# Pair scores of eight GLA heads: the levels within 32 tokens as 32x32 blocks in one round

## The chip, the cores and the metric

One core of a Trainium2 chip runs the whole program in one launch. The metric is the device time of one execution in microseconds (us), the median of several runs. TensorE is written PE, VectorE DVE, ScalarE ACT, GpSimd POOL, and SyncE, which issues most DMAs, SP.

## The reference, cut to what matters

The model is a two-layer streaming encoder: 1024 prompt tokens and 8 x 16 sample tokens, width 1024. Layer 0 mixes tokens with two recurrences side by side, a gated DeltaNet and a GLA (gated linear attention) with 8 heads of key width 32 and value width 64. The change concerns the pairwise part of GLA inside one block of tokens:

```python
b = jnp.cumsum(gc, axis=2)
diff = b[:, :, :, None, :] - b[:, :, None, :, :]
decay = jnp.exp(jnp.where(causal[:, :, None], diff, -jnp.inf))
a = jnp.einsum('bhid,bhjd,bhijd->bhij', qc, kc, decay)
o = o_inter + jnp.einsum('bhij,bhje->bhie', a, vc)
```

For each pair of a query i and a key j not after it the score is the sum over 32 channels of q, k and a decay that depends on both and on the channel. `o_inter` is what comes from the carried state. All data are float32.

## The kernel before, in words

The program runs in stages. The one touched is the stage of the recurrences (`recurrences`, L3047, with `mixer_out` behind it), from about 440 to 880 us of the span. It takes the 1152 tokens in nine tiles of 128: first the sample tile (`order`, L3058), then eight prompt tiles.

**Software pipeline.** Each engine's program is written out by hand, turn by turn (`each`, L3210). Turn i handles three tiles: tile i gets the inverse of its DeltaNet matrix and its GLA pairs, tile i+1 (called n) is prepared, and tile i-1 (s) makes outputs and new states. Turns 1 to 7 have the same shape, turn 0 belongs to the sample tile, and turn 8 is written out as `last_turn`, where work of the next part (`ahead`) stands between the steps. Every engine executes in order; engines meet in semaphores, wrapped as `Tally` objects that count per tile.

**GLA pairs by levels.** Because the decay depends on the channel, scores can't come from one product. For each of seven levels s = 1, 2, 4, ..., 64 (`LEVELS`; NL is their number) queries and keys are scaled to a common midpoint (`level_queries` on DVE, `level_keys` on POOL). The level s product is right for pairs in which the key lies in the lower half and the query in the upper half of a group of 2s tokens; index NL stands for the diagonal, made of unscaled queries and keys. So every level is a 128x128 product of which a mask keeps some blocks. Levels 1 to 16 and the diagonal keep elements only inside the four 32x32 diagonal blocks; level 32 (index 5) keeps two whole 32x32 blocks off the diagonal, level 64 (index 6) one 64x64 block. A sample tile, whose streams are 16 tokens long, needs only levels 1 to 8 and the diagonal.

**PE, `pairs` (L3536, product L3553).** One job is one level: 8 matmuls, each contracting 32 rows (a head's channels) against 128 columns, 4 heads side by side in the four row groups of the array, into PSUM banks 4 to 7 (a bank per head of four). A round holds one or two jobs:

```python
rounds_p, rounds_s = [[0, 1], [2, 3], [4, NL], [5, 6]], [[0, 1], [2], [3], [NL]]
```

**DVE, `place` (L4073).** After each round it moves what the masks keep into `gla_pairs` (`ga`, two copies by turn parity): `copy_predicated` over all 128x1024 elements for a level with a mask (L4093), plain copies for level 32 (L4090, two) and level 64 (L4087, one). Round r+1 of `pairs` waits until round r is placed, since both use the same banks. The buffer is zeroed once at the start of the stage (L4020), as elements above or below the kept blocks stay zero.

**The order in a turn around the change.** PE: `turn_qk(n, 1)`, `pairs` round 0, `du_quarters`, one unit of cached keys transposed (`turn_keys`), `turn_qk(n, 2)`, another unit of keys, `z_half` (L3526), `pairs` round 1, `du_half` (L3533), `a_pairs(n)` (L3457), `pairs` round 2, `p_pairs(n)` (L3457), `pairs` round 3, `turn_w` (L3563), `exponents(n)` (L3479). Turn i+1 begins with `z_blocks` (L3496) and, for prompt tiles, `values` (L3621), which needs the exponentials of `exponents(n)` that ACT makes (L3820). DVE: `place` round 0, `merge32` (L4046, L4048), `place` round 1, `merge64` (L4052), `decayed(n)` (L4058), `place` round 2, `pairs_decayed(n)` (L4066), `place` round 3, `set_blocks(n)`. ACT: `keep_keys`, `keep_z_half` (L3838), `bt_blocks(n)` (L3889), `keep_w` (L3901), `level_exps(n)`.

Who waits for whom: `z_half` needs `merge32`; `turn_w` needs `merge64`; `p_pairs` and `bt_blocks` need `decayed`; `exponents` reuses banks 4 to 7 and needs the last `place`. `gla_outputs` (L3647) of tile i reads `gla_pairs` in turn i+1. Small blocks have a neighbour in the same stage: the inverse works on 32x32 blocks too (`z_blocks` L3496, `du_blocks` L3503: 32 matmuls of 32x32 each; `put`, L4033: `copy_predicated` over 128x256 elements with the masks `upc`, L4034). The reads of the sample states (`sample_reads`, L3582) put GLA matmuls with 32 rows and 32 columns on all 16 tiles of the array.

A float32 matmul has two records in the profile, so 32 matmuls are x64 there.

## Time and profile before

| | |
|---|---|
| median of 3 runs | 3221.96 us (3221.78 to 3223.81) |
| the profiled execution | 3232.05 us |
| its span | 3230.4 us |
| busy: PE, DVE, ACT, POOL | 3093.9, 1578.8, 1029.4, 1527.5 us |
| `pairs` matmuls (L3553) | 1104 records |
| `place` with a mask (L4093) | 53, 1300 ns each |
| `place` copies (L4090, L4087) | 16 of 417 ns, 8 of 682 ns |

Times in the profile are us from the start of the span, unless marked ns. In a timeline a line is one instruction or a merged run of equal ones, with its start and length; brackets at its end give the idle time of the engine before it and what ended that. The granted clock of PE is given as a share of full speed: 1.00 is 2.4 GHz, 0.50 is 1.2 GHz.

### The profile page before, as it was taken

The numbers are of one execution on the slowest core, as the hardware profiler recorded it, in microseconds if no ns is written. First come the engines' busy times: TensorE is split into PE (matmuls) and PEld (weight loads), VectorE is DVE, ScalarE is ACT, GpSimd is POOL, SyncE is SP. The second block draws the span as 40 slices with busy tenths as digits, with TensorE's granted clock in tenths as the row PEclk, the third lists the DMA queues.
The fourth block names the chain that finished last, engine by engine and source line by source line (L and its number), as shares of the span: only waits on it lengthen the run. The fifth ranks groups of instructions, "written<-read, shape, count | busy, mean of one in ns | idle before, by whom it ended". The sixth has DMA issues, their size and how long they took to land. (4 is left out here: it accounts for less than half of the span.)

```text
span 3230.4 us, 67257 instructions
## 1 busy us (share of the span) xinstructions
PE 3093.9 (96%) x28484; PEld 2905.2 (90%) x28484; DVE 1578.8 (49%) x2177; ACT 1029.4 (32%) x1834; POOL 1527.5 (47%) x1163
## 2 busy tenths in 40 slices
PE   7999987888898999999999999999999999999999
PEld 6988876777798999999999999877699999999998
DVE  5650034565566545554334433466646445553323
ACT  4222132333434332231212432356624332231112
POOL 4452324344115776674363556311126766764352
PEclk8999988999898999999999999999999999999999
DMA  6222142432651322236423353567521333238342
GB/s 208 83 79 98 59 135 65 146 127 98 212 188 56 97 99 79 94 120 255 146 94 138 93 155 116 171 212 240 155 77 64 103 97 103 78 111 303 98 141 79
DMA packets 371080, 409.45 MB, mean 127 GB/s; under 512 B 29048, under 2 KB 303569, under 8 KB 369768
## 3 DMA queue, kind: packets, MB, share of 16 engines
q1 hardware_dynamic: 363944, 380.24, 35.5%
q0 software_dynamic: 6848, 25.04, 2.5%
q8 instruction: 222, 3.64, 0.5%
q14 instruction: 66, 0.54, 0.1%
HBM read 272.71 MB, written 134.60 MB: 126 GB/s over the span
## 5 line engine op out<-in xcount | busy, mean ns | idle before, releaser
L864 PE MATMUL PS<-token_block,w_block 128*128 128x288 f32 x9408 | 1272.3, 297 | 13.6 <-POOL w_block L778 6.5
L864 PEld LDWEIGHTS PS<-token_block,w_block 128*128 128x128 f32 x9408 | 1264.0, 190 | 16.2 <-POOL w_block L778 6.1
L778 POOL TENSOR_TENSOR w_block<-w_pair_raw,w_block 128x512 fp32r<-128x512 f32 x224 | 303.2, 1360 | 163.2 <-ACT w_block L774 129.2
L1259 PE MATMUL PS<-act_slot,w_down_split 128*128 128x384 f32 x1872 | 330.4, 337 | 6.6 <-DMA act_slot<-act_dram 5.5
L1259 PEld LDWEIGHTS PS<-act_slot,w_down_split 128*128 128x128 f32 x1872 | 328.1, 189 | 8.2 <-DMA act_slot<-act_dram 6.4
L778 POOL TENSOR_TENSOR w_block<-w_sum,w_block 128x512 fp32r<-128x512 f32 x168 | 228.7, 1376 | 96.9 <-ACT w_block L774 96.8
L774 ACT CAST w_block<-w_pair_raw 128x512 fp32r<-128x512 f32 x224 | 137.7, 622 | 306.6 <-PE PS L864 265.2
L774 ACT CAST w_block<-w_sum 128x512 fp32r<-128x512 f32 x168 | 99.5, 621 | 366.2 <-POOL w_sum L767 235.6
L1231 PE MATMUL PS<-token_block,w_block 128*128 128x288 f32 x1344 | 180.4, 296 | 2.1 <-issue 2.1
L1231 PEld LDWEIGHTS PS<-token_block,w_block 128*128 128x128 f32 x1344 | 179.4, 189 | 3.0 <-issue 2.5
L762 POOL TENSOR_TENSOR w_sum<-w_pair_raw 128x512 f32<-128x512 f32 x56 | 87.9, 1570 | 166.4 <-DMA w_pair_raw<-in_ffn_w_gu_dram 112.0
L405 PE MATMUL PS<-hT_high,w_split_tiles 128*128 128x384 f32 x576 | 124.9, 342 | 2.6 <-DVEq L2468 2.6
L1090 POOL CAST w_down_split<-w_down_raw 128x1024 fp32r<-128x1024 f32 (+2 forms) x32 | 28.1, 878 | 207.7 <-PE PS L1259 172.6
L1555 DVE TENSOR_TENSOR xT<-xT,PS 128x1152 f32<-128x1152 f32 x32 | 43.3, 1354 | 155.5 <-PE PS L1259 155.5
L1481 DVE TENSOR_TENSOR u<-p,PS 128x576 f32<-128x576 f32 x44 | 33.1, 752 | 164.9 <-PE PS L864 164.9
L4968 ACT ACTIVATE probs<-minus_scores,minus_max 128x640 f32<-128x640 f32 (+3 forms) x144 | 101.3, 707 | 23.5 <-DVE minus_max L4857 23.2
L1546 DVE TENSOR_TENSOR xT<-xT,PS 128x576 f32<-128x576 f32 x72 | 52.6, 752 | 106.3 <-PE PS L1231 106.3
L3395 POOL TENSOR_TENSOR gla_k_exps<-gla_exps,gla_kT 128x896 f32<-128x896 f32 x18 | 37.1, 2083 | 142.3 <-ACT gla_exps L3820 142.3
L405 PEld LDWEIGHTS PS<-hT_high,w_split_tiles 128*128 128x128 f32 x576 | 101.4, 190 | 2.9 <-POOLq L2338 2.9
L5005 POOL COPY bias_samples<-bias_near 128x384 f32<-128x384 f32 x16 | 8.1, 504 | 195.7 <-DMA bias_near<-near_dram 171.9
L764 POOL TENSOR_TENSOR w_sum<-w_sum,w_pair_raw 128x512 f32<-128x512 f32 x56 | 98.4, 1757 | 4.4
L1497 DVE TENSOR_TENSOR ffn_up<-ffn_up,norm_row 128x1152 f32<-128x1152 f32 x44 | 94.1, 2138 | 4.6
(520 smaller groups left out, 5516.3 us busy)
## 6 DMA issues: line engine op xcount, KB each, us to landing
w_pair_raw<-in_ffn_w_gu_dram SPq DMA_DIRECT2D x88, 512.0 KB, 5.1
act_slot<-act_dram SPq DMA_DIRECT2D x28, 1152.0 KB, 13.0
cache_kT<-kT_dram SPq DMA_DIRECT2D x8, 2048.0 KB, 11.6
cache_v<-in_cache_c_v_dram SPq DMA_DIRECT2D x64, 256.0 KB, 4.8
act_dram<-ffn_act_high SPq DMA_DIRECT2D x28, 576.0 KB, 2.8
act_dram<-ffn_act_low SPq DMA_DIRECT2D x28, 576.0 KB, 3.9
down_source<-down_dram SPq DMA_DIRECT2D x56, 288.0 KB, 5.2
xT<-xT_dram SPq DMA_DIRECT2D x24, 576.0 KB, 12.0
```

The lines of the kernel that those rows point to most:

```text
L405: m = nc.tensor.matmul(PS[:, banks + j, 0:GN], wl if p == 2 else wh, sl if p == 1 else sh, start=(k == first and p == 0), stop=(k == last ...
L762: tt(self.sum_(p, 2), b0, b1, ALU.add).then_inc(self.summed, 1)
L764: tt(self.sum_(p, 1), self.sum_(p, 2), a0, ALU.subtract).then_inc(self.summed, 1)
L774: self.nc.scalar.copy(self.blocks[q][:, 0], self.source(p, q)).then_inc(self.high, 1)
L778: self.nc.gpsimd.tensor_tensor(self.blocks[q][:, 1], self.source(p, q), self.blocks[q][:, 0], ALU.subtract).then_inc(self.low, 1)
L864: m = nc.tensor.matmul(to[:, j], w, x[:, j * HN:(j + 1) * HN], start=(q < 3 and i == 0 and t == 0), stop=(q > 3 and i == 3 and t == 2), sk ...
L1231: m = nc.tensor.matmul(to[:, j], w, x[:, j * HN:(j + 1) * HN], start=(q < 3 and i == 0 and t == 0), stop=(q > 3 and i == 3 and t == 2), sk ...
L1259: m = nc.tensor.matmul(down_banks(u)[:, j], wd[u % 2][:, int(q == 2), k], x[:, int(q == 1), group(j)], start=(k == 0 and q == 0), stop=(k ...
L1497: tt(up[:], up[:], row[:], ALU.mult).then_inc(up_scaled, 1)
L1546: tt(two(x), two(x), down_tile(d, q), ALU.add).then_inc(x_down, 1)
L1555: tt(groups(xT[:, n]), groups(xT[:, n]), down_banks(u), ALU.add).then_inc(x_added, 1)
L4968: nc.scalar.activation(pr[:, g % 2, hp, 0:w], sc[:, hp, 0:w], ACT.Exp, scale=-1.0, bias=mn[:, g % 2, hp, 0:1], accum_out=sm[:, g % 2, hp, ...
```

## The change

Jobs 0 to 4 and the diagonal (NL) become one round. Each of them is now 32 matmuls of 32 rows by 32 columns with 32 moving columns (for each of 2 halves of heads, 4 key blocks b and 4 heads), and all of them together fill 384 columns of banks 4 to 7. DVE selects them with six `copy_predicated` of 128x256 elements into a compact buffer `gc`, one after the other, each waiting for the one before it. ACT then copies the four diagonal blocks to their place in `gla_pairs` (`spread_pairs`, four copies of 32x256 elements), after `keep_z_half` and before `bt_blocks`. Levels 32 and 64 stay as they were and are the second and last round; rounds 2 and 3 of a prompt tile are gone, and so are the steps for them in PE's and DVE's orders. `turn_w` now stands ahead of `p_pairs`. For the sample tile the rounds are levels 1 to 8, and the diagonal. New waits: `gla_outputs` waits for the spreading of its tile, `place` round 0 for that of the tile before, and ACT's `spread_pairs` for the first round placed (for the sample tile for both). One more `memset` stands at the start of the stage.

```diff
--- before.py
+++ after.py
@@ -73,7 +73,7 @@
     u["up"] = np.concatenate(up + [np.eye(P) > 0], 1)
     r, q = row % 32, np.arange(32)[None, :]
     u["upc"] = np.concatenate([(r // (2 * s) == q // (2 * s)) & (r % (2 * s) < s) & (q % (2 * s) >= s)
-                               for s in LEVELS[:5]], 1)
+                               for s in LEVELS[:5]] + [r == q], 1)
     where, n = {}, 0
     for k, v in f.items():
         where[k] = (n, n + v.shape[1])
@@ -3056,7 +3056,7 @@
     Q = 32
     B = P // Q
     order = [NPT] + list(range(NPT))
-    rounds_p, rounds_s = [[0, 1], [2, 3], [4, NL], [5, 6]], [[0, 1], [2], [3], [NL]]
+    rounds_p, rounds_s = [[0, 1, 2, 3, 4, NL], [5, 6]], [[0, 1, 2, 3], [NL]]
     NK = PAST // P
     NU = CH // 2 * BS // 2
     cache_k = d["cache_c_k"][0].rearrange("b r h c -> b r (h c)")
@@ -3100,6 +3100,7 @@
     ql = sb("gla_q_exps", [P, 2, NL, P])
     kl = sb("gla_k_exps", [P, 2, NL, P])
     ga = sb("gla_pairs", [P, 2, H, P])
+    gc = sb("gla_pair_blocks", [P, H, Q])
     qt = sb("qT", [P, 3, H // 2, P])
     kt = sb("kT", [P, H // 2, P])
     kbt = sb("kbT", [P, H // 2, P])
@@ -3150,7 +3151,8 @@
     l32_put, t64_ready, diag_put = tally("merge32_put"), tally("first_half_ready"), tally("diagonal_put")
     z64_mm, z64_kept, du64_mm, u_done = tally("z64_mm"), tally("z64_kept"), tally("du64_mm"), tally("inverse_done")
     gs_high, gs_split = tally("gla_g_high"), tally("gla_g_low")
-    pairs_mm, ga_put = tally("gla_pairs_mm", 4), tally("gla_pairs_put", 4)
+    ga_spread = tally("gla_blocks_spread")
+    pairs_mm, ga_put = tally("gla_pairs_mm", 2), tally("gla_pairs_put", 2)
     wt_mm, wt_ready = tally("wt_mm"), tally("wt_ready")
     v_mm, v_ready, qs_mm, qs_scaled = tally("v_mm"), tally("v_ready"), tally("qs_mm"), tally("qs_scaled")
     o_mm, o_ready, go_mm, go_kept = tally("o_mm"), tally("o_ready"), tally("go_mm"), tally("go_kept")
@@ -3547,10 +3549,17 @@
             jobs = (rounds_s if sample(k) else rounds_p)[r]
             for x, j in enumerate(jobs):
                 for m in range(2):
-                    for h in range(4):
-                        rows = slice(GK * h, GK * h + GK)
-                        w, q = (gkt[:, k % 2, m], gqt[:, k % 2, m]) if j == NL else (kl[:, m, j], ql[:, m, j])
-                        y = mm(PS[:, 4 + h, x * 256 + m * P:x * 256 + (m + 1) * P], w[rows], q[rows], start=True, stop=True)
+                    w, q = (gkt[:, k % 2, m], gqt[:, k % 2, m]) if j == NL else (kl[:, m, j], ql[:, m, j])
+                    if j in (NL - 2, NL - 1):
+                        for h in range(4):
+                            rows = slice(GK * h, GK * h + GK)
+                            y = mm(PS[:, 4 + h, x * 256 + m * P:x * 256 + (m + 1) * P], w[rows], q[rows], start=True, stop=True)
+                        continue
+                    for b in range(B):
+                        for h in range(4):
+                            rows = slice(GK * h, GK * h + GK)
+                            y = mm(PS[quad(b), 4 + h, (x * 2 + m) * Q:(x * 2 + m + 1) * Q], w[rows, quad(b)], q[rows, quad(b)],
+                                   start=True, stop=True)
             y.then_inc(pairs_mm.sem, 1)
 
         def turn_w(k):
@@ -3600,6 +3609,7 @@
 
         def sample_gla_outputs(k):
             pe.wait_ge(v_in[k % 3], 16 * (k // 3 + 1))
+            ga_spread.wait(pe, k)
             v_ready.wait(pe, k)
             qs_scaled.wait(pe, k)
             o_ready.wait(pe, k)
@@ -3646,6 +3656,7 @@
 
         def gla_outputs(k):
             pe.wait_ge(v_in[k % 3], 16 * (k // 3 + 1))
+            ga_spread.wait(pe, k)
             gs_added.wait(pe, k - 1)
             for m in range(2):
                 mm(PS[:, 7, m * 256:(m + 1) * 256], qe[:, k % 3, m], GS[:, m].rearrange("p h v -> p (h v)"),
@@ -3734,8 +3745,6 @@
             du_half(i)
             pe.wait_ge(keys_kept, NU)
             ahead.turn(pe, 0)
-            pairs(i, 2)
-            pairs(i, 3)
             turn_w(i)
             ahead.turn(pe, 1)
 
@@ -3805,13 +3814,9 @@
                 du_half(i)
             if n is not None:
                 a_pairs(n)
-            if i is not None:
-                pairs(i, 2)
-            if n is not None:
+            if n is not None and i is not None:
+                turn_w(i)
                 p_pairs(n)
-            if i is not None:
-                pairs(i, 3)
-                turn_w(i)
             if n is not None:
                 exponents(n)
         each(turn)
@@ -3888,6 +3893,12 @@
             for b in range(B):
                 x = copy(btc[quad(b)], bt[k % 2][quad(b), :, quad(b)])
             x.then_inc(btc_ready.sem, 1)
+
+        def spread_pairs(k):
+            ga_put.wait(act, k, 1 if not sample(k) else 2)
+            for b in range(B):
+                x = copy(ga[quad(b), k % 2, :, quad(b)], gc[quad(b)])
+            x.then_inc(ga_spread.sem, 1)
 
         def keep_w(k):
             wt_mm.wait(act, k)
@@ -3958,6 +3969,7 @@
             keep_keys(i, 5)
             keep_keys(i, 6)
             keep_z_half(i)
+            spread_pairs(i)
             keep_keys(i, 7)
             ahead.high(act, 0)
             ahead.square(act, 2)
@@ -4005,6 +4017,7 @@
             if i is not None:
                 keep_keys(i, 2)
                 keep_z_half(i)
+                spread_pairs(i)
             if n is not None:
                 bt_blocks(n)
             if i is not None:
@@ -4018,6 +4031,7 @@
         tt_ = v.tensor_tensor
         v.memset(u[:], 0.0)
         v.memset(ga[:], 0.0)
+        v.memset(gc[:], 0.0)
         v.memset(wts[:], 0.0).then_inc(zeroed, 1)
 
         def set_blocks(k):
@@ -4074,23 +4088,28 @@
             pairs_mm.wait(dve, k, r + 1)
             if r == 0:
                 go_mm.wait(dve, k - 2)
+                ga_spread.wait(dve, k - 1)
             if r == 0 and k < 2:
                 dve.wait_ge(zeroed, 1)
-            to = ga[:, k % 2].rearrange("p (h m) t -> p h m t", m=2)
             jobs = (rounds_s if sample(k) else rounds_p)[r]
             ga_put.wait(dve, k if r else -1, r)
+            to = ga[:, k % 2].rearrange("p (h m) t -> p h m t", m=2)
+            within = gc[:].rearrange("p (h m) t -> p h m t", m=2)
             for x, j in enumerate(jobs):
                 if x:
-                    dve.wait_ge(ga_half, firsts(k, r) + 1)
-                src = PS[:, 4:8, x * 256:(x + 1) * 256].rearrange("p h (m t) -> p h m t", m=2)
+                    dve.wait_ge(ga_half, firsts(k, r) + x)
+                if j in (NL - 2, NL - 1):
+                    src = PS[:, 4:8, x * 256:(x + 1) * 256].rearrange("p h (m t) -> p h m t", m=2)
                 if j == NL - 1:
                     y = v.tensor_copy(to[0:64, :, :, 64:P], src[0:64, :, :, 64:P])
                 elif j == NL - 2:
                     for b in (0, 2):
                         y = v.tensor_copy(to[quad(b), :, :, quad(b + 1)], src[quad(b), :, :, quad(b + 1)])
                 else:
-                    mask = c("up")[:, j * P:(j + 1) * P].rearrange("p (a b t) -> p a b t", a=1, b=1)
-                    y = v.copy_predicated(to, bc(mask, (P, 4, 2, P)), src)
+                    n = min(j, 5)
+                    mask = c("upc")[:, n * Q:(n + 1) * Q].rearrange("p (a b t) -> p a b t", a=1, b=1)
+                    src = PS[:, 4:8, x * 2 * Q:(x + 1) * 2 * Q].rearrange("p h (m t) -> p h m t", m=2)
+                    y = v.copy_predicated(within, bc(mask, (P, 4, 2, Q)), src)
                 y.then_inc(ga_put.sem if x == len(jobs) - 1 else ga_half, 1)
 
         def factors(k):
@@ -4204,9 +4223,7 @@
             place(i, 1)
             merge64(i)
             ahead.low(dve, 0)
-            place(i, 2)
             ahead.sums(dve, 2)
-            place(i, 3)
             ahead.gate(dve, 2)
 
         def turn(i, n, s):
@@ -4244,13 +4261,7 @@
                 merge64(i)
             if n is not None:
                 decayed(n)
-            if i is not None:
-                place(i, 2)
-            if n is not None:
                 pairs_decayed(n)
-            if i is not None:
-                place(i, 3)
-            if n is not None:
                 set_blocks(n)
         each(turn)
 
@@ -4680,7 +4691,7 @@
           ("k_normed", 2048), ("k_beta", 2048), ("dn_states", 8192), ("tile_gla_v", 6144), ("qT", 6144),
           ("inverse_T", 8192), ("gla_pairs", 8192), ("z_halves", 2048), ("inverse_first_half", 2048), ("qk_pairs", 8192),
           ("inverse_blocks", 1024), ("z_blocks", 1024), ("sample_q_exp", 2048), ("egl", 384),
-          ("head_gains", 32), ("o_ss", 128), ("o_eps", 32), ("small_exps", 192), ("first_factors", 64))
+          ("head_gains", 32), ("o_ss", 128), ("o_eps", 32), ("small_exps", 192), ("first_factors", 64), ("gla_pair_blocks", 1024))
     stack(rest, ("mix_rows", 8192), ("gate_rows", 8192), ("o_sq", 4096))
     at_["x_sq"] = consts + 4096
     states, v, q, u, p, g = (at_[k] for k in ("dn_states", "tile_gla_v", "qT", "inverse_T", "qk_pairs", "gla_pairs"))
```

## Rows read from the trace of the kernel before

**Rows 1.** Busy time by windows: window, us, each engine, PEclk, DMA share, GB/s

```profile
640.00:684.50 44.50, 38.76 (x958) 33.17 (x959) 26.73 (x42) 17.33 (x35) 19.56 (x16) 1.00 0.35 115
...
509.90:511.60 1.70, 1.70 (x129) 1.58 (x133) 0.00 (x0) 0.00 (x0) 0.00 (x0) 0.50 0.00 0
...
527.00:533.00 6.00, 5.98 (x93) 5.15 (x92) 3.64 (x5) 3.82 (x8) 3.48 (x5) 0.50 0.65 182
```

**Rows 2.** Timeline of PE in one prompt turn: start us, us, engine, line, records [idle before]

```profile
654.45 0.75 PE L3503 MATMUL PS<-inverse_T_blocks,z_blocks 32*32 32x32 f32 x64
...
663.62 1.17 PE L3553 MATMUL PS<-gla_q_exps,gla_k_exps 32*128 32x128 f32 x32 [0.51 <-DVE gla_state L4162]
...
667.64 1.06 PE L3702 MATMUL PS<-consts_f,sample_qT 128*128 128x128 f32 x8 [0.42 <-ACT sample_wT L3937]
...
668.83 1.11 PE L3526 MATMUL PS<-inverse_first_half,minus_aT_even 64*64 64x64 f32 x16
...
669.87 1.17 PE L3553 MATMUL PS<-gla_q_exps,gla_k_exps 32*128 32x128 f32 x32
...
672.05 1.16 PE L3457 MATMUL PS<-kbT,kT 64*128 64x128 f32 x16
...
675.50 1.16 PE L3457 MATMUL PS<-qT,kT 64*128 64x128 f32 x16 [0.50 <-DVE minus_aT_odd L4058]
...
678.03 1.17 PE L3553 MATMUL PS<-gla_q_exps,gla_k_exps 32*128 32x128 f32 x32 [1.38 <-DVE gla_pairs L4093]
...
679.14 1.09 PE L3563 MATMUL PS<-inverse_T,minus_k_beta_eg 128*64 128x128 f32 x16
...
680.89 0.50 PE L3479 MATMUL PS<-spans_r,gla_g_split 128*128 128x512 f32 x1 [0.66 <-DVE gla_pairs L4087]
...
684.52 1.97 PE L3621 MATMUL PS<-v_beta,inverse_T 128*128 128x64 f32 x16 [0.63 <-ACT gla_exps L3820]
```

**Rows 3.** Timeline of DVE in the same turn

```profile
664.85 2.68 DVE L4093 COPY_PREDICATED gla_pairs<-consts_u,PS 128x1024 f32<-128x1024 uint8 x2 [1.53 <-PE PS L3553]
...
667.43 0.83 DVE L4046 COPY inverse_T<-PS 32x256 f32<-32x256 f32 x2
...
668.27 0.42 DVE L4048 COPY inverse_first_half<-PS 32x256 f32<-32x256 f32 x1
...
673.65 0.66 DVE L4052 COPY inverse_T<-PS 64x512 f32<-64x512 f32 x1
...
674.25 1.20 DVE L4058 SCALAR_TENSOR_TENSOR minus_aT_odd<-PS,decay 128x1024 f32<-128x1024 f32 x1
```

**Rows 4.** Timeline of ACT in the same turn

```profile
675.48 1.65 ACT L3889 COPY minus_aT_blocks<-minus_aT_odd 32x256 f32<-32x256 f32 x4 [4.91 <-DVE minus_aT_odd L4058]
```

**Rows 5.** By source line: engine, op, count: ns min/median/max

```profile
L3503 PE MATMUL PS<-inverse_T_blocks,z_blocks x2304: 184/191/258, 443.7 to 839.5; 32*32 32x32 f32 x192
...
L4034 DVE COPY_PREDICATED inverse_T_blocks<-consts_u,PS x36: 431/444/451, 445.9 to 839.7; 128x256 f32<-128x256 uint8 x36
```

**Rows 6.** Timeline of PE, small-tile groups at the lower clock

```profile
457.79 1.07 PE L3503 MATMUL PS<-inverse_T_blocks,z_blocks 32*32 32x32 f32 x64 [0.49 <-ACT z_blocks L3826]
...
509.96 1.87 PE L3582 MATMUL PS<-gla_states,sample_q_exp 32*32 32x64 f32 x122
```

**Rows 7.** Timeline of PE, the same part in turns 0 and 1

```profile
466.13 2.09 PE L3553 MATMUL PS<-gla_q_exps,gla_k_exps 32*128 32x128 f32 x32
...
481.36 0.50 PE L3479 MATMUL PS<-spans_r,gla_g_split 128*128 128x512 f32 x1 [0.74 <-DVE gla_pairs L4093]
...
527.14 2.09 PE L3553 MATMUL PS<-gla_q_exps,gla_k_exps 32*128 32x128 f32 x32
...
547.40 0.50 PE L3479 MATMUL PS<-spans_r,gla_g_split 128*128 128x512 f32 x1
```

**Rows 8.** Timeline of PE in the last turn

```profile
843.82 1.78 PE L3553 MATMUL PS<-gla_q_exps,gla_k_exps 32*128 32x128 f32 x32
...
871.23 2.04 PE L3621 MATMUL PS<-v_beta,inverse_T 128*128 128x64 f32 x16
```

## The prediction, made before the result was known

> **What bounds the kernel now.** I began with the busy times of the stage by windows [rows 1]. In a prompt turn of 44.5 us PE works 38.8, DVE 26.7, ACT 17.3 and POOL 19.6, with PE at its upper clock, 2.4 GHz (granted 1.00). So PE leads the stage and only what it does or waits for counts. The timeline of PE shows where its waits lie [rows 2]. From `pairs` round 0 (663.62) to `exponents` (680.89) pass 17.27 us, and three of the waits there end with DVE work on the pairs or behind it: 0.50 before `p_pairs`, 1.38 before round 3, 0.66 before `exponents`. The timeline of DVE [rows 3] shows why: two masked selections of one round take 2.68 us, and `merge32`, `merge64` and `decayed` stand in the same queue. The start of `values` then hangs on the exponentials, 3.63 us behind `exponents` (684.52). The turn is a chain with PE and DVE taking turns; a shortened piece shortens the turn. All seven turns 1 to 7 are built so; turn 1 has part of it at the lower clock.
>
> **PE: what the products cost.** Removed per prompt tile: six of eight jobs, or 96 of the 128 records of four rounds, a round of 32 taking 1.17 [rows 2]. Added: 6 jobs of 32 matmuls, 384 records of 32x32x32. No row shows that order of tiles at the upper clock. The nearest is `du_blocks`: 64 records in 0.75 [rows 2], with 0.19 for one record [rows 5]; less the last one's own length that is 0.56/63 = 8.9 ns a record. If the whole 0.75 is charged it is 11.7. These use four tiles on the array's diagonal; the new order walks down the four row groups of one column strip, then goes to the next. `sample_reads` does the same, at the lower clock (granted 0.50, [rows 1]): 122 records in 1.87, at most 15.3 ns each, against 1.07/64 = 16.7 for the diagonal order at that clock [rows 6]. So the order of tiles costs nothing that shows. I take 8.9 and 0.1 for the start: round 0 lasts 3.5 us, with 11.7 it lasts 4.5; at the lower clock, with (1.07 - 0.26)/63 = 13 ns (0.26 is the longest single record, [rows 5]), 5.0. Against the four old rounds (4.6 together) PE's own work stays about equal: 3.5 and the last round, 1.17.
>
> The Trainium skill has a rule against this change (TensorE: Matmul & The Clock Gate, section "Wait — 56ns, not 53.3ns?"): however small a matmul, the next one starts no sooner than about 25 ns after it. The trace disagrees a little if a float32 matmul, with its two records, is one: 2 x 8.9 = 17.8 ns. By that rule round 0 would be 192 x 25 = 4.8 us, an estimate from that page, and a turn would gain 1.3 less than below.
>
> **DVE.** Removed: six masked selections of 128x1024, 2.68 for two [rows 3], 8.0 in all. Added: six of 128x256 at 0.444 [rows 5]; each waits for the one before, some 0.03 as between the two old ones, so 2.85. DVE is freed of 5.2 us, but only where PE waited for it does that count.
>
> **ACT.** Added: four copies of 32x256, like those of `bt_blocks`, 1.65 [rows 4]. They stand where ACT now idles 4.91 before `bt_blocks`, so I cost them at nothing. The cover: `z_half` comes at 7.95 (below), its result is kept by 9.6 and the spreading ends at 11.3; `bt_blocks` can start at 13.5. Without that cover they would cost 1.65 a turn, as `keep_w` and the exponentials queue behind. Their reader, `gla_outputs`, comes in the next turn; DVE's new wait (round 0 for the spreading of the tile before) is as old. In the sample tile the spreading waits for round 1 as well, and `bt_blocks`, `keep_w` and the exponentials are queued behind it, still in time. No DMA moves; POOL and SP are only passed by the shift. SP's stores of keys, and the loads of the next ones behind them, come up to 2.5 us later in a turn; their reader is PE in the next turn.
>
> **The turn, walked through.** Times from the start of round 0.
> - Round 0 ends at 3.5; with the step to DVE 3.65. Six selections: 6.5. `merge32` 0.83 + 0.42 [rows 3]: 7.75. PE meanwhile does `du_quarters`, two units of keys (1.06 each, with ACT's copy between) and `turn_qk`; that ends near 7.6 and is just hidden. `z_half` starts at 7.9, where before it started at 5.21 (668.83). So this part gets 2.7 worse.
> - `z_half`, round 1 and `du_half` take 672.05 - 668.83 = 3.2: `a_pairs` at 11.1, done at 12.3. DVE places levels 32 and 64 from 10.1 (two 32x256 and one 64x512, 0.83 + 0.66 by like copies [rows 3]) to 11.6, `merge64` to 12.3, `decayed` 1.20 to 13.5.
> - `turn_w` (1.09) fits ahead of that. `p_pairs` 13.6 to 14.7. No round follows, so `exponents` starts at 14.7 against 17.27 before.
>
> **Gain: 2.5 us in each of turns 2 to 7.** `values` follows by the same 3.6, since ACT is through with `bt_blocks` (13.5 + 1.65) and `keep_w` before the exponents land. With 11.7 ns a record it is 1.5.
>
> **The other turns** [rows 7, 8]. Turn 1 took 547.40 - 527.14 = 20.26 for the same part, as PE ran at 0.50 from 527 to about 533 [rows 1] and its round 0 took 2.09. Now round 0 takes 5.0 there; 14.7 - 3.5 + 5.0 = 16.2, a gain of 4.0. Turn 0 (sample) took 481.36 - 466.13 = 15.23, with four jobs in round 0: 256 records, 3.1 at a mix of clocks, 1.9 for four selections, 1.25 `merge32`; here the second unit of keys comes last and `z_half` starts near 7.0, then 3.2 + 3.3: 13.5, a gain of 1.7. From it goes the new memset, a quarter of a microsecond by its size. The last turn runs mostly at the lower clock and takes 27.41 to `values`; round 0 costs 5.0, the waits for rounds 2 and 3 go, but the rows of the next part are loaded only after a transpose that now comes some 2 us later. Between 0 and 2.5 I take 1.
>
> **Sum:** 6 x 2.5 + 4.0 + 1.5 + 1.0 = 21.5 us. Behind the stage PE is dense and nothing is tied to a fixed time, so the shift passes to the end. The profiled execution took 3232.05, 10 us above the median of 3221.96, and would come to 3210.5; the median to **3200.5 us**.
>
> **Rivals.**
> 1. *Dense price, faster all the same.* At 11.7 ns a record turns 2 to 7 gain 1.5, turn 1 some 2.5, turn 0 and the last one 0.5 together: 12 us, 3210. For it: 0.75 is what the whole group takes. Against: it charges the tail 64 records at a time. The skill's floor would land here too, at about 3209. Chance 0.22.
> 2. *Given back.* Another wait takes over, such as keys' transposes, `merge32` or the spreading of ACT ahead of `keep_w`: a piece of 1.65 or more a turn is lost and under 6 us remain, about 3218. For it: PE and ACT are just hidden before `z_half` in my walk. Against: ACT's 4.91 of idle. That the edit doesn't do what it says falls in here. Chance 0.10.
> 3. *Slower through the clock.* PE falls to 1.2 GHz within the turns, because 384 tiny products replace wide ones, or because PE now waits longer in one piece. Price: a wide round takes 2.09 for 1.17 [rows 7, 2], so each microsecond at the lower level loses 0.44; the gain of 2.5 is gone at 5.7 us a turn. If the whole part of 14.7 ran there in turns 2 to 7, 6 x (6.5 - 2.5) = 24 are lost: 3240. For it: PE was at 0.50 in early stretches with many small products. Against: DVE's waits within the turn shrink, and PE has other work while DVE selects. Chance 0.08.
> 4. *Slower through the array.* If row groups over one column strip did not run side by side, a record would cost up to four times 8.9, 36 ns, and round 0 some 13.7: a loss of 7.7 a turn, 3280. It decides from (3.5 + 2.5)/384 = 15.6 ns on. Against: the 15.3 of `sample_reads`, with twice the columns and at half the clock [rows 6]. Chance 0.05, most of it for lesser slowdowns.
>
> **The numbers.** A measurement of this kernel tells 0.2% (6.4 us) from nothing. My forecast has 0.55, rival 1 0.22, both faster: 0.77. Within 0.2%: 0.10, rival 2. Slower: 0.13, rivals 3 and 4. The range goes from 3193 (the clock stays up in turn 1 and the last turn, a record costs 8 ns) to 3218, through rivals 1 and 2; left out are the slower ones and some of both ends.
>
> **What would show it.** Round 0 near 3.5 us with 384 records; selections of 0.44 each; `z_half` some 7.9 us after the start of round 0, `exponents` 14.7 after it; turns of 42.0 instead of 44.5; ACT's spreading ahead of `bt_blocks` with idle time left between them; the stage about 21 us shorter. Round 0 above 6 us, a granted clock under 1.00 in turns 2 to 7, or a wait of PE for `gla_pairs` in the next turn would make it wrong.

## The result: slower by 2.7%, and the profile after

The changed kernel takes 3308.13 us in the median (3300.32 to 3322.85, four runs), the kernel before 3222.89 in the same set. The ratio is 1.0271, with an interval of 1.0248 to 1.0293. Forecast were 3200.5 us, 3193 to 3218: wrong in sign, by 108 us.

The page of the changed kernel, its first lines and the queue that brings instructions (packets, MB, share of 16 engines):

```profile
span 3321.2 us, 72364 instructions
...
PE 3122.4 (94%) x31028; PEld 2935.6 (88%) x31028; DVE 1550.6 (47%) x2178; ACT 1041.3 (31%) x1870; POOL 1521.4 (46%) x1163
...
q8 instruction: 242, 3.96, 0.5%
```

For the kernel before the queue's line reads:

```profile
q8 instruction: 222, 3.64, 0.5%
```

The stage as one window, from its start almost to its end, for the changed kernel and then for the one before (columns as in [rows 1]; PE's first product of the part that follows starts at 962.12 and at 881.83):

```profile
435.00:958.00 523.00, 405.02 (x11557) 352.70 (x11558) 213.10 (x387) 178.54 (x348) 170.00 (x131) 0.79 0.37 116
```

```profile
435.00:880.00 445.00, 376.01 (x9037) 321.63 (x9035) 255.50 (x389) 165.84 (x314) 170.11 (x131) 0.91 0.42 133
```

In these windows the stage grew from 445 to 523 us, up to that first product by 80. PE works 405.0 for 376.0 us, with 2520 records more, and DVE 42 us less. So 49 of the 78 us are idle time of PE, and 29 are work, part of it at the lower clock: the granted clock of the stage fell from 0.91 to 0.79. What lies behind the stage took 10.5 us longer than in the profile of before; no run here explains that part.

The timeline of PE in a turn that answers to [rows 2], from round 0 on (the line of the small products is L3561 now, `z_half` is L3528, `exponents` L3481; rows between left out):

```profile
692.65 1.28 PE L3561 MATMUL PS<-gla_q_exps,gla_k_exps 32*32 32x32 f32 x128 [0.46 <-DVE gla_state L4181]
...
696.20 1.53 PE L3561 MATMUL PS<-gla_q_exps,gla_k_exps 32*32 32x32 f32 x128 [2.27 <-issue]
...
702.95 0.82 PE L3561 MATMUL PS<-gla_q_exps,gla_k_exps 32*32 32x32 f32 x60 [5.22 <-issue]
...
703.59 0.89 PE L3561 MATMUL PS<-gla_qT,gla_kT 32*32 32x32 f32 x62
706.40 0.26 PE L3520 MATMUL PS<-inverse_T_blocks,z_blocks 32*32 32x32 f32 x2 [1.93 <-issue]
...
712.43 1.97 PE L3528 MATMUL PS<-inverse_first_half,minus_aT_even 64*64 64x64 f32 x16
...
718.25 2.08 PE L3459 MATMUL PS<-kbT,kT 64*128 64x128 f32 x16
...
723.74 0.50 PE L3481 MATMUL PS<-spans_r,gla_g_split 128*128 128x512 f32 x1
```

Round 0 does not last 3.5 us but until about 704.5, some 12; in the eight prompt turns it lasts 9.3 to 13.7. It comes in pieces: 128 records in 1.28 us, a pause of 2.27, 128 records in 1.53, a pause of 5.22, and the last 128 (their line is cut where the tile's name changes). A pause of 1.93 follows in `du_quarters` (L3520). The pauses end with "issue": PE waits for nothing that another engine does. `exponents` starts 31.1 us after round 0, where before it was 17.27 [rows 2]. Within a piece the records are as fast as forecast: (1.28 - 0.19)/127 = 8.6 ns each in the first one. In the six turns in which `values` of before follows itself after 44.4 to 44.6 us, it now does after 48.2 to 58.3, 54.7 on average.

The windows over those pieces and pauses, with the loads that SP issues in them:

```profile
692.00:694.00 2.00, 1.46 (x130) 1.19 (x129) 0.38 (x2) 1.93 (x6) 2.00 (x3) 1.00 0.07 16
...
694.00:696.20 2.20, 0.00 (x1) 0.00 (x1) 0.00 (x0) 1.45 (x4) 2.12 (x4) 0.94 0.88 279
...
696.20:698.00 1.80, 1.53 (x128) 1.39 (x128) 0.00 (x0) 0.00 (x0) 0.16 (x1) 0.50 0.81 226
...
698.00:703.00 5.00, 0.06 (x9) 0.05 (x12) 0.00 (x0) 0.00 (x0) 0.00 (x0) 0.50 0.44 166
```

```profile
693.24 0.34 SPq L3225 DMA_DIRECT2D tile_qkv<-qkv_dram  x1
...
693.68 1.42 SPq L3228 DMA_DIRECT2D tile_gla_qk<-rest_dram  x1
...
695.21 0.35 SPq L3235 DMA_DIRECT2D tile_gla_v<-rest_dram  x1
```

The granted clock is at 1.00 in the first piece, 0.94 on average over the pause behind it and 0.50 from then on; the DMA share is 0.88 in that pause and 0.44 in the long one.

What the change does on the other engines is as forecast. A selection of DVE, by source line, and the spreading by ACT in the same turn, right behind `keep_z_half`:

```profile
L4112 DVE COPY_PREDICATED gla_pair_blocks<-consts_u,PS x53: 439/443/447, 466.7 to 931.4; 128x256 f32<-128x256 uint8 x53
```

```profile
715.04 1.64 ACT L3900 COPY gla_pairs<-gla_pair_blocks 32x256 f32<-32x256 f32 x4
```

0.443 us for 0.444 [rows 5], and 1.64 for 1.65 [rows 4].

### The profile page after: what moved, and what is told of

It reads as the page before. It is cut to its first block and busy times, and to the rows that moved or that the text cites. A ratio compares the mean times of both kernels' runs of the same rounds, so it can differ in the third digit from the quotient of the medians.

```text
span 3321.2 us, 72364 instructions
## 1 busy us (share of the span) xinstructions
PE 3122.4 (94%) x31028; PEld 2935.6 (88%) x31028; DVE 1550.6 (47%) x2178; ACT 1041.3 (31%) x1870; POOL 1521.4 (46%) x1163
```

## The experiments

Three theories. *Instruction supply*: PE's instructions are fetched in blocks, and a long burst of 10 ns matmuls uses them up faster than they come. What spoke for it at once: the pieces are 128 records long; the queue q8 moved 20 packets and 0.32 MB more, 16 KB a packet; and 2520 records of PE more, with a weight load each, are 20 blocks of 256 instructions. The whole count fits too: 28484 records with a weight load each are 222.5 such blocks, and the queue moved 222 packets before; 31028 records are 242.4, and it moved 242 after. *Array*: row groups over one column strip disturb each other (rival 4). *New waits*: what ACT and DVE now wait for holds PE (rival 2).

The same trace also holds the time of each packet. Before every pause of over 1.5 us in or behind round 0 of a prompt turn ends, one packet of 16 KB of that queue has landed 1.2 to 1.6 us earlier. In the long pause above (697.73 to 702.95) it started only at 700.53 and took 0.88 us. The DMA view of 696.20 to 700.40 has no packet of q8, that of 696.20 to 703.00 has one (packets, MB, share):

```profile
q1 hardware_dynamic: 457, 1.17, 82.7%
```

```profile
q1 hardware_dynamic: 476, 1.22, 52.8%
q8 instruction: 1, 0.02, 0.8%
```

**1. Another order of tiles (a_diag).**

```diff
-                    for b in range(B):
+                    for d_ in range(B):
                         for h in range(4):
+                            b = (h + d_) % B
```

> The changed kernel, with round 0 in another order of tiles: four matmuls in a row take four different row groups and four different column strips, as the products of the inverse do. Theory 'instruction supply' (the instructions of PE arrive in blocks, slower than matmuls of 10 ns use them up): the same count, so the same idle time without a releaser inside round 0, some 9 us a turn, and 3300 to 3320 us. Theory 'array' (row groups over one column strip disturb each other): the pauses vanish, about 3200 to 3215 us. Theory 'new waits' (the waits for spreading and for the compact buffer hold DVE and ACT, and PE behind them): 3300 to 3320, with the pauses outside round 0.

Measured: 3300.07 us, ratio 1.0249 (1.0207 to 1.0290). The pauses are as before, again between pieces of 128 records:

```profile
642.17 1.27 PE L3562 MATMUL PS<-gla_q_exps,gla_k_exps 32*32 32x32 f32 x128 [0.59 <-issue]
...
649.75 1.08 PE L3562 MATMUL PS<-gla_q_exps,gla_k_exps 32*32 32x32 f32 x83 [6.30 <-issue]
...
653.48 0.33 PE L3562 MATMUL PS<-gla_qT,gla_kT 32*32 32x32 f32 x16 [2.21 <-issue]
```

The array theory falls: with a different row group and column strip for each matmul nothing changes that counts. The new waits would have given the same time, but with the pauses outside round 0; they are inside.

**2. The same round with fewer, wide matmuls (a_wide).** The scores within 32 tokens are not computed as wanted; everything else stays.

```diff
-                    for b in range(B):
-                        for h in range(4):
-                            rows = slice(GK * h, GK * h + GK)
-                            y = mm(PS[quad(b), 4 + h, (x * 2 + m) * Q:(x * 2 + m + 1) * Q], w[rows, quad(b)], q[rows, quad(b)],
-                                   start=True, stop=True)
+                    for h in range(4):
+                        rows = slice(GK * h, GK * h + GK)
+                        y = mm(PS[:, 4 + h, (x * 2 + m) * Q:(x * 2 + m) * Q + P], w[rows], q[rows], start=True, stop=True)
```

> The changed kernel with round 0 as wide matmuls again: 8 instead of 32 per job, each 32 rows by 128 columns with 128 moving columns, written to overlapping columns of the same banks (so the scores within 32 tokens are not those wanted). All of the change on DVE and ACT and all waits stay. Round 0 has 96 records for 384 and should last 3.3 us at the upper clock, about what was forecast for the small ones. Instruction supply: no pauses in round 0, turns of about 42 us, 3198 to 3210 us. Array: the same. New waits: still 3300 or so.

Measured: 3200.6 us (3196.62 to 3206.04, seven runs), ratio 0.9935 (0.9916 to 0.9954). PE, DVE and ACT in one of its turns (L3560 round 0, L3528 `z_half`, L3481 `exponents`; L4110 the selections, L3898 the spreading, L3892 `bt_blocks`):

```profile
610.63 2.51 PE L3560 MATMUL PS<-gla_q_exps,gla_k_exps 32*128 32x128 f32 x80 [0.46 <-DVE gla_state L4179]
...
617.81 1.11 PE L3528 MATMUL PS<-inverse_first_half,minus_aT_odd 64*64 64x64 f32 x16 [0.31 <-DVE inverse_first_half L4060]
...
624.61 0.50 PE L3481 MATMUL PS<-spans_r,gla_g_split 128*128 128x512 f32 x1
```

```profile
613.64 2.85 DVE L4110 COPY_PREDICATED gla_pair_blocks<-consts_u,PS 128x256 f32<-128x256 uint8 x6 [3.27 <-PE PS L3560]
```

```profile
619.56 1.64 ACT L3898 COPY gla_pairs<-gla_pair_blocks 32x256 f32<-32x256 f32 x4
...
623.49 1.65 ACT L3892 COPY minus_aT_blocks<-minus_aT_even 32x256 f32<-32x256 f32 x4 [2.29 <-DVE minus_aT_even L4070]
```

Round 0 lasts 2.96 us (the other 16 records, of the diagonal, follow under another tile's name), near the 3.5 that I had given the small products, and all behind it goes as in the walk: `z_half` at 7.2 us (forecast 7.9), `exponents` at 14.0 (14.7), six selections in 2.85, the spreading with idle time behind it. So neither the new waits nor DVE or ACT cost anything. A turn takes 41.1 us. What the changed kernel loses comes with the 384 small products. That it is their number and not their shape is shown by the 8.6 ns within a piece and by the queue of instructions: it moves 222 packets here, as before the change.

**3. Fewer jobs (a_two).** Round 0 multiplies its first two jobs only.

```diff
+                    if x >= 2:
+                        continue
                     for b in range(B):
```

> The changed kernel with only the first two jobs of round 0 multiplied (128 records for 384 in a prompt tile; the products of the other levels within 32 tokens are left out, DVE selects as many times as before). Instruction supply: little or no pause, as a burst of 128 is about what already exists in the kernel; round 0 lasts 1.3 us, turns of 40 to 41 us, 3180 to 3200 us. Array: a third of the loss stays, some 3220. New waits: above 3280.

Measured: 3226.13 us (3216.11 to 3232.67), ratio 1.0020 (1.0000 to 1.0040). A miss: faster than the changed kernel by 82 us, but not below 3200, and nearer to what stood there for the array theory, which the first run had ruled out. PE's pauses without a releaser add up to 26 us in the stage, where a_wide has 11 and the changed kernel 81. The first product behind the stage starts 18.6 us later than in a_wide; PE's idle time explains 12 of that and its work 7, at a granted clock of 0.86 for 0.92. The longest such waits stand right behind the 128 records, in `du_quarters` (9.7 us in four waits). So 128 small records are enough there to be short of a block. Why here, where other bursts of 128 pass, was not tested.

**4. A burst in the kernel before (b_burst).**

```diff
-            for h in range(H):
-                for b in range(B):
-                    x = mm(blocks(0)[quad(b), h], zc[quad(b), h], uc[quad(b), h], start=True, stop=True)
+            for again in range(6 if l == 0 else 1):
+                for h in range(H):
+                    for b in range(B):
+                        x = mm(blocks(0)[quad(b), h], zc[quad(b), h], uc[quad(b), h], start=True, stop=True)
```

> The kernel before, with the first set of 32 products of the inverse in a turn (du_blocks, level 0, on the diagonal tiles) multiplied six times over, each time with the same result. That makes bursts of 384 records in another place, with nothing else changed. By their rate they cost 320 x 8.9 ns = 2.8 us a turn, 26 us in nine tiles: 3250. Instruction supply: pauses without a releaser of some 5 to 10 us a turn show inside or right behind them as well, 3290 to 3340 us. Array and new waits: none, 3245 to 3255 us.

Measured: 3313.72 us, ratio 1.0277 (1.0238 to 1.0317): nothing of the change, and as large a loss. Some 26 us of the 93 are the price of the added records by the rate above; PE's pauses without a releaser add up to 52 us in the stage, for 14 in the kernel before, and its granted clock is 0.86 for 0.91. PE's timeline in two turns, and a window with its DMA share (the last column but one):

```profile
625.32 1.59 PE L3504 MATMUL PS<-inverse_T_blocks,z_blocks 32*32 32x32 f32 x165
628.91 1.27 PE L3504 MATMUL PS<-inverse_T_blocks,z_blocks 32*32 32x32 f32 x128 [2.00 <-issue]
...
632.37 1.49 PE L3504 MATMUL PS<-inverse_T_blocks,z_blocks 32*32 32x32 f32 x91 [2.19 <-issue]
...
682.59 1.89 PE L3504 MATMUL PS<-inverse_T_blocks,z_blocks 32*32 32x32 f32 x128 [1.95 <-issue]
...
686.05 1.60 PE L3504 MATMUL PS<-inverse_T_blocks,z_blocks 32*32 32x32 f32 x100 [1.58 <-issue]
```

```profile
629.00:633.00 4.00, 1.81 (x176) 1.70 (x179) 0.00 (x0) 0.00 (x0) 2.37 (x3) 0.81 0.01 4
```

Again the piece in the middle has 128 records; how many come before the first pause differs from turn to turn (here 165). From one piece's start to the next pass 632.37 - 628.91 = 3.46 us at one place and 686.05 - 682.59 = 3.46 at another, with next to no other transfers. The packets of the instruction queue around the first place start at 626.53, 630.03 and 633.51 and take about 1 us each. That is the pace at which blocks of 256 instructions come in quiet: 13.5 ns an instruction, 27 ns a record with its weight load, where a 32x32 matmul needs 8.9.

**5. Loads out of the way (a_late).** SP loads the tile after next only behind round 0.

```diff
             kd_ready.wait(sp, k - 1)
+            pairs_mm.wait(sp, k - 2, 1)
             sp.dma_start(lq[:], qkv[r]).then_inc(q_in.sem, 16)
```

> The changed kernel; SP issues the loads of the tile after next (1.25 MB with the values) only when round 0 of this turn is multiplied, where they now start inside it. Instruction supply, with the blocks competing with these loads (pauses of 5 to 6.6 us under a DMA share of 0.9, of 2.0 in the burst of b_burst under 0.01): pauses fall to some 2 us each, 5 us a turn less, 3255 to 3275 us. Supply at a fixed rate: no change, 3300.

Measured: 3287.45 us, ratio 1.0203 (1.0174 to 1.0232). In a turn the pieces now follow at 3.46 and 3.47 us:

```profile
634.90 1.53 PE L3562 MATMUL PS<-gla_q_exps,gla_k_exps 32*32 32x32 f32 x128 [2.80 <-issue]
...
638.36 1.08 PE L3562 MATMUL PS<-gla_q_exps,gla_k_exps 32*32 32x32 f32 x83 [1.93 <-issue]
...
641.83 0.33 PE L3562 MATMUL PS<-gla_qT,gla_kT 32*32 32x32 f32 x14 [1.93 <-issue]
```

So other transfers do delay the blocks: with the loads moved behind the burst, the pauses within round 0 are 0.5 to 2.8 us in turns 1 to 7, where the changed kernel has one of 4.7 to 6.6 in six of the seven. PE's pauses in the stage fall from 81 to 61 us, and the time by about as much, 21 us. A miss by size: I expected 33 to 53, with 5 us less in a turn, and a turn got 3.0 shorter.

How they delay them shows in the trace of the changed kernel. In the six long pauses the packet of instructions itself took 0.9 to 1.0 us, no longer than in quiet, but it started late: at 700.53 in the turn above, 4.3 us after the start of the piece before, where in quiet it is 1.1 (630.03 behind 628.91 in b_burst). In five of the six it started just when the other transfers ran out (in the turn above 14 to 16 packets were under way 1 to 3 us ahead of it, 2 right behind its start); in the sixth (646.62) 15 were still under way.

**6. The products spread (a_spread, a_spread_late).** Round 0 in four pieces between wider work, `merge32` ahead of the selections, levels 32 and 64 behind `a_pairs`; then with the late loads as well.

```diff
+                pairs(i, 0, (0, 1))
                 du_quarters(i)
                 turn_keys(i, 1)
+                pairs(i, 0, (2,))
                 turn_qk(n, 2)
+                pairs(i, 0, (3,))
                 turn_keys(i, 2)
                 z_half(i)
+                pairs(i, 0, (4, 5))
                 du_half(i)
                 a_pairs(n)
+                pairs(i, 1)
```

> The changed kernel with the same products, but those of round 0 in four pieces (two jobs, one, one, two) between the transposes, with merge32 on DVE ahead of the selection, and levels 32 and 64 behind a_pairs. Supply: blocks come while wide work runs; at one block per 3.3 us in quiet the 4.4 blocks of this part fit in its 14 to 18 us only if the loads leave room; 3215 to 3260 us. Pauses by the array or the waits: 3290 or more.

> Both of these. Supply with competition: 3200 to 3235 us, with pauses of under 3 us a turn. If it comes out as a_spread alone does, competition plays no part.

Measured: 3290.63 us, ratio 1.0215 (1.0188 to 1.0242), and 3267.59, ratio 1.0135 (1.0100 to 1.0171). Both come out above their ranges, though in the right order. For a_spread the time even falls where I had put the rivals, 3290 or more; that they are not the cause rests on a_diag and a_wide, and on the pauses, which still have no releaser. Pauses remain in the spread kernel, such as this one:

```profile
651.95 0.36 PE L3563 MATMUL PS<-gla_q_exps,gla_k_exps 32*32 32x32 f32 x15 [3.05 <-issue]
```

Spreading cuts the pauses without a releaser from 81 us in the stage to 47, and to 37 with late loads. The time of a_spread falls by only 18, as PE's work in the stage grows, from 409 to 426 us up to the first product behind it, at a granted clock of 0.78; with late loads it is 402 at 0.85. That the loads and the keys' transfers are what keeps the rest of the pauses was not tested.

**7. Blocks of 64x64 (a_64, a_64_late).** 240 records a tile for the pairs, in two rounds of four jobs, spread.

```diff
-    rounds_p, rounds_s = [[0, 1, 2, 3, 4, NL], [5, 6]], [[0, 1, 2, 3], [NL]]
+    rounds_p, rounds_s = [[0, 1, 2, 3], [4, NL, 5, 6]], [[0, 1, 2, 3], [NL]]
...
+                    for b in range(2 if j != NL - 1 else 1):
+                            y = mm(PS[64 * b:64 * b + 64, 4 + h, (x * 2 + m) * 64:(x * 2 + m + 1) * 64],
+                                   w[rows, 64 * b:64 * b + 64], q[rows, 64 * e_:64 * e_ + 64], start=True, stop=True)
```

> Another cut of the same change: blocks of 64x64, so 16 matmuls of 32 rows by 64 columns with 64 moving columns per job (8 for level 64), 240 records a tile for 128 before and 416 in the changed kernel, in two rounds of four jobs, spread as in a_spread; DVE selects 128x512 elements (0.73 us each by its rate of 1300 ns for 1024 and 444 for 256), ACT copies two blocks of 64x512. Supply: few pauses; exponents 13 to 14 us after the start of round 0, 3190 to 3215 us. Were tile sizes as such the cause: above 3240.

> The 64x64 cut with the loads of SP behind its first four jobs. If competition with the loads is what keeps it from the 14 us of its walk: 3205 to 3218 us. If the blocks of instructions come too slowly even in quiet (one per 3.46 us in b_burst and a_late), or DVE's selections bound it: as a_64, 3222.

Measured: 3222.29 us, ratio 1.0002 (0.9980 to 1.0024), and 3232.55, ratio 1.0026 (1.0010 to 1.0043). PE and DVE in a turn of a_64:

```profile
657.57 0.90 PE L3561 MATMUL PS<-gla_q_exps,gla_k_exps 32*64 32x64 f32 x64 [0.47 <-DVE gla_state L4180]
...
672.12 0.50 PE L3483 MATMUL PS<-spans_r,gla_g_split 128*128 128x512 f32 x1 [0.96 <-DVE gla_pairs L4107]
```

```profile
662.15 3.03 DVE L4111 COPY_PREDICATED gla_pair_blocks<-consts_u,PS 128x512 f32<-128x512 uint8 x4 [1.72 <-PE PS L3561]
```

`exponents` starts 14.55 us after the first piece, not far from the 13 to 14 expected, and pauses are back at 14 us in the stage, with 32-row tiles still in use. Both times miss their ranges. Turns 2 to 7 are 1.4 us shorter than before on average, and the profiled stage is 13.3 shorter; 5.4 of that are given back behind it. The 7.9 that are left don't show in the medians, for the profiled execution of before happened to be 9.5 above its median in this set and that of a_64 only 1.8. Late loads bring the pauses to 24 us in the stage; why was not followed further.

**8. Relief for DVE without a matmul more (b_act).** The kernel before, with levels 32 and 64 as round 1, placed by ACT, and the rounds moved forward.

```diff
-    rounds_p, rounds_s = [[0, 1], [2, 3], [4, NL], [5, 6]], [[0, 1], [2], [3], [NL]]
+    rounds_p, rounds_s = [[0, 1], [5, 6], [2, 3], [4, NL]], [[0, 1], [2], [3], [NL]]
...
+        def place_far(k):
+            pairs_mm.wait(act, k, 2)
+            for b in (0, 2):
+                copy(to[quad(b), :, :, quad(b + 1)], src[0][quad(b), :, :, quad(b + 1)])
+            y = copy(to[0:64, :, :, 64:P], src[1][0:64, :, :, 64:P])
+            y.then_inc(ga_put.sem, 1)
```

> The kernel before with its wide products, no record more for PE: levels 32 and 64 become round 1, placed by ACT (two copies of 32x256, one of 64x512, 1.5 us) in place of DVE, round 2 before du_half, round 3 before turn_w, p_pairs behind both. By the walk through the turn exponents starts 15.7 us after round 0 for 17.3, 1.6 us a turn: 3208 to 3216 us. If ACT's copies delay the keys or keep_z_half more than the walk says, no change.

Measured: 3210.40 us (3201.20 to 3216.31, twelve runs) against 3223.15, ratio 0.9961 (0.9945 to 0.9977). This one beats both kernels, the one before by 0.4%. PE and ACT in a turn:

```profile
610.93 1.17 PE L3553 MATMUL PS<-gla_q_exps,gla_k_exps 32*128 32x128 f32 x32 [0.46 <-DVE gla_state L4176]
...
626.26 0.50 PE L3479 MATMUL PS<-spans_r,gla_g_split 128*128 128x512 f32 x1 [0.94 <-DVE gla_pairs L4107]
...
629.88 1.97 PE L3621 MATMUL PS<-v_beta,inverse_T 128*128 128x64 f32 x16 [0.59 <-ACT gla_exps L3819]
```

```profile
616.14 0.74 ACT L3898 COPY gla_pairs<-PS 32x256 f32<-32x256 f32 x2 [0.84 <-PE PS L3553]
...
616.89 0.58 ACT L3899 COPY gla_pairs<-PS 64x512 f32<-64x512 f32 x1
```

`exponents` starts 15.3 us after round 0 (forecast 15.7, before 17.27), and ACT's copies take 0.74 and 0.58. A turn takes 42.5 us for 44.4.

## Why the prediction was wrong

**The step that failed** is the price of the products: "I take 8.9 and 0.1 for the start: round 0 lasts 3.5 us", and its upper end of 11.7 ns a record. The 8.9 was right for what it was read from, a burst of 64 records, and within the first piece of round 0 it holds (8.6). It does not carry to 384 in a row. There the blocks of instructions set the pace, 27 ns a record at best and 53 with transfers beside (6.75 us from 696.20 to 702.95 for 128 records; 61 in the turn before). With 27 the walk would have given 384 x 27 = 10.4 us for round 0, seven more a turn, and the sign would have been right, though not the size. In the turn shown `exponents` comes 16.4 us later than in the walk: 8.3 of them lie in round 0, 3.5 between it and `z_half` (1.9 is the pause in `du_quarters`), and 4.5 from `z_half` on, where the same work runs at a granted clock of 0.50.

**The trace of before had the warning.** Its waits list, in the stage, has idle time of PE with no releaser at three lines with small matmuls, and the most at the 128x128 transposes of L3702 (idle time summed in us, waits, the longest):

```profile
PE PS L3702 <- issue: 4.0, 3, 2.3
...
PE PS L3503 <- issue: 3.6, 3, 2.0
...
PE PS L3496 <- issue: 2.6, 2, 2.3
...
PE PS L3582 <- issue: 2.1, 1, 2.1
```

The timeline of before has one such place in the sample's part:

```profile
491.38 1.17 PE L3582 MATMUL PS<-dn_states,sample_qT 64*32 64x64 f32 x96 [2.11 <-issue]
492.48 0.58 PE L3496 MATMUL PS<-inverse_blocks,minus_aT_blocks 32*32 32x32 f32 x32
495.39 0.65 PE L3496 MATMUL PS<-inverse_blocks,minus_aT_blocks 32*32 32x32 f32 x32 [2.33 <-issue]
```

96 and 32 records, 128 together, stand between two pauses without a releaser. I read the waits that end with DVE and left these out. The 2.11 are in `sample_reads` (L3582), the function from whose later reads, at 509.96 [rows 6], I took that tile order costs nothing; I took the pace within that group and did not look at what happens to several hundred small records in a row.

**The rest of the walk** held. a_wide has the same edit on DVE and ACT with few instructions of PE, and its 3200.6 us stand beside my 3200.5 for the whole. That they agree so closely is luck. In the profiles its turns 2 to 7 gain 3.3 us each for 2.5, the last turn 2.3 for 1.0, turns 0 and 1 together 5.1 for 5.5, and the whole execution 26 for 21.5; the medians differ by 20.2, as the profiled executions lie above them by different amounts.

**The rivals.** Rival 4 set the point of decision right, 15.6 ns a record, and named the wrong cause: a_diag shows that the array is not it, and b_burst has the loss without that order. Rival 3, the clock, is real as a second step: PE falls to 0.50 in the pauses and runs on there into the next products, as `z_half` at 712.43 with 1.97 for 1.11 us [rows 2]. The tiny products did not bring it about, for the first piece runs at 1.00 throughout; a longer wait of PE in one piece, the other way that the rival named, fits, but it is the wait for instructions. From its start to the first product behind it the stage exceeds that of a_wide by 104 us: 64 are idle time of PE and 40 its work, at the slower clock and with the added records. The pauses without a releaser alone are 70 us more; PE's other waits are shorter. Rival 2 fell with a_wide. Rival 1, the dense price, was of the right kind and far too small.

The Trainium skill has the rule that I needed and did not weigh (Runtime: NRT & Kernel Launch, section "Instruction fetch mechanics"): an engine's instructions come through a FIFO, refilled in blocks of 16 KiB or 256 instructions by a DMA queue of its own. The traces agree on the block: pieces of 128 records, 16 KB a packet. The same section says that the fetch is hidden, as instructions are dispatched more slowly than they arrive. For bursts of small matmuls the measurements decide otherwise: 3.46 us a block in quiet against 1.28 us to use it up.

## What to carry to other kernels

Count the instructions of a burst on PE, not only its columns: when several hundred tiny matmuls stand in a row, the price of 128 float32 records is what their block of 256 instructions costs to fetch, 3.46 us here and about twice that beside heavy loads. Before cutting wide products into small ones, look in the waits list for idle time with the releaser "issue" at lines that already have small tiles, and count the records between two such waits. Relief for another engine is worth taking where it costs PE no instruction, as in b_act.

## What the runs showed of the hardware

- PE's instructions came in blocks of 256 (128 matmul records and their weight loads; 222 packets of 16 KB for 28484 records before, 242 for 31028 after). In quiet, pieces of 128 records followed each other every 3.46 us, also where PE's granted clock was at 0.50 (b_burst at 682.59). A packet took about 1 us of that and landed 1.2 to 1.6 us before the piece that it was needed for.
- Beside other transfers a block took longer: the pauses reached 4.7 to 6.6 us in the changed kernel, with the loads of the next tile issued in the burst, and were at most 2.8 in the same turns when those loads were moved (a_late). The packet was not slower, it started later, mostly when the other transfers ran out.
- The reserve in front of PE was small: a burst paused after its first 82 to 218 records in the changed kernel and after 32 to 266 in b_burst. The 96 wider records of a_wide's round 0 never paused.
- In the changed kernel's round 0 the granted clock stood at 1.00 in the first piece, 0.94 in the pause of 2.27 us behind it and 0.50 from then on, and `z_half` in that turn took 1.97 us for 1.11.
